# Gated recurrence of a twelve-plus-four sublayer network: weight splits ahead of the next pair's sigmoid, the last pair's output products by column halves, and the next sublayer's first splits during the last mean square

## The reference, cut to what matters

```python
q, zf, zb, i, g = jnp.split(h @ w_in, 5, axis=-1)      # h is the normed x, w_in is 1024 x 5120
k_f, logf_f = forget(zf)                               # forget: a bounded sigmoid of z
k_b, logf_b = forget(zb)
o = forward_scan(q, k_f, v, logf_f) + backward_scan(q, k_b, v, logf_b)    # 8 heads of 128
o = _rms_norm(o, g_norm) * jax.nn.silu(gh)             # the mean square is over one head's 128 features
return o.reshape(B, T, D_MODEL) @ w_out                # w_out is 1024 x 1024
```

## Time and profile before

| what | value |
|---|---|
| launches, median (lowest to highest) | 3114.99 us (3114.23 to 3117.01) |
| the profiled launch: its own time, its span | 3116.85 us, 3115.0 us |
| instructions in the profile | 46410 |
| PE busy | 2902.4 us, 93% of the span |
| PE's share of the chain of work that ended last | 83% (DVE 9%, ACT 4%) |
| DVE busy | 1998.4 us, 64% |
| ACT busy | 1425.0 us, 46% |
| mean granted clock of PE over the span | 0.964 of full |
| the two recurrences, from the first pair's first score to the last product with `w_out` | 193.0 us and 192.9 us |

### The profile page before, as it was taken

How to read it: one execution, slowest core, us unless ns; L and a number is a source line. 1 busy time by engine, 2 the same in 40 slices (tenths; PEclk the granted TensorE clock), 3 DMA queues, 4 the chain that set the end, 5 groups by cost and what they waited for, 6 DMA issues and landing times.

```text
span 3115.0 us, 46410 instructions
## 1 busy us (share of the span) xinstructions
PE 2902.4 (93%) x19567; PEld 2643.7 (85%) x19567; DVE 1998.4 (64%) x2593; ACT 1425.0 (46%) x1891; POOL 83.2 (3%) x135
## 2 busy tenths in 40 slices
PE   7999889999989999999799999997999789896998
PEld 7999879999976999995489999986899689794897
DVE  5657766566657656553665665677666677746777
ACT  4445544444444444442554444554444445343453
POOL 0000000000011000000000000000000000000000
PEclk9999989999999999999999999998999889997999
DMA  6554336575532655642146566432564455542552
GB/s 231 183 163 136 115 97 201 176 216 183 160 104 61 214 186 183 184 117 86 61 141 185 169 198 188 149 122 89 163 185 157 157 165 176 163 150 81 163 188 97
DMA packets 404051, 478.24 MB, mean 154 GB/s; under 512 B 16394, under 2 KB 331492, under 8 KB 403844
## 3 DMA queue, kind: packets, MB, share of 16 engines
q1 hardware_dynamic: 400432, 467.33, 48.0%
q0 software_dynamic: 1776, 6.77, 0.8%
q10 hardware_dynamic: 1636, 1.18, 0.1%
HBM read 474.17 MB, written 1.05 MB: 153 GB/s over the span
## 4 chain that ended last, share of the span: by engine, by line
PE 83%; DVE 9%; ACT 4%; issue 3%; ACTq 0%; DVEq 0%
PE Wk L569 16%; PE Wk L571 16%; PE Wk L570 16%; PE Y L569 9%; PE Y L570 9%; PE Y L571 9%; DVE w_lo L1608 2%; PE Wk L577 2%; DVE work L1846 2%; ACT w_hi L1133 1%; PE Y L926 1%; PE Y L681 1%; PE Wk L899 1%; PE Y L829 1%; PE Wk L915 1%
## 5 line engine op out<-in xcount | busy, mean ns | idle before, releaser
L1608 DVE TENSOR_TENSOR w_lo<-ring,w_hi 128x1024 fp32r<-128x1024 f32 x872 | 1046.8, 1223 | 680.5 <-ACT w_hi L1133 634.2
L569 PE MATMUL Wk<-xT_hi,w_hi 128*128 128x256 f32 x4320 | 1234.3, 286 | 19.2 <-DVE xT_lo L1646 16.0
L571 PE MATMUL Wk<-xT_hi,w_lo 128*128 128x256 f32 x4320 | 1226.3, 284 | 0.0
L570 PE MATMUL Wk<-xT_lo,w_hi 128*128 128x256 f32 x4320 | 1226.3, 284 | 0.0
L1133 ACT ACTIVATE w_hi<-ring 128x1024 fp32r<-128x1024 f32 x872 | 896.6, 1053 | 644.4 <-PE Wk L571 432.6
L569 PEld LDWEIGHTS Wk<-xT_hi,w_hi 128*128 128x128 f32 x4320 | 832.9, 193 | 26.5 <-issue 13.0
L570 PEld LDWEIGHTS Wk<-xT_lo,w_hi 128*128 128x128 f32 x4320 | 833.0, 193 | 4.7 <-issue 0.9
L571 PEld LDWEIGHTS Wk<-xT_hi,w_lo 128*128 128x128 f32 x4320 | 832.6, 193 | 0.0
L569 PE MATMUL Y<-w_hi,hid_hi 128*128 128x512 f32 x896 | 352.4, 393 | 4.3 <-DVE hid_lo L1700 4.3
L570 PE MATMUL Y<-w_lo,hid_hi 128*128 128x512 f32 x896 | 351.0, 392 | 0.0
L571 PE MATMUL Y<-w_hi,hid_lo 128*128 128x512 f32 x896 | 349.8, 390 | 0.0
(11 more groups left out here) (250 smaller groups left out, 2796.9 us busy)
## 6 DMA issues: line engine op xcount, KB each, us to landing
ring<-in_ffn_w_gu SPq DMA_DIRECT2D x352, 512.0 KB, 4.4
ring<-in_ffn_w_down SPq DMA_DIRECT2D x224, 512.0 KB, 4.4
ring<-in_ffn_w_up SPq DMA_DIRECT2D x96, 512.0 KB, 6.0
ring<-in_hg_w_in SPq DMA_DIRECT2D x80, 512.0 KB, 3.6
ring<-in_na_w_in SPq DMA_DIRECT2D x24, 512.0 KB, 4.5
ring<-in_hg_w_out SPq DMA_DIRECT2D x16, 512.0 KB, 3.7
ring<-in_lru_w_in SPq DMA_DIRECT2D x16, 512.0 KB, 4.0
ring<-in_kv_w SPq DMA_DIRECT2D x16, 512.0 KB, 4.7
```

Source lines behind the costliest of these rows:

```text
L569: pe.matmul(o, l_hi, r_hi, start=first, stop=False)
L570: pe.matmul(o, l_hi, r_lo, start=False, stop=False)
L571: return pe.matmul(o, l_lo, r_hi, start=False, stop=last)
L1608: dve.tensor_tensor(lo, raw(u), hi.bitcast(F32), ALU.subtract).then_inc(lo_done, 1)
```

## The change

Six things are edited, all for the recurrence:

1. On ACT and DVE, in pairs 0 to 2, `ahead` moves from the end of a round to just after the scores' own steps: on ACT before `squares_of`, `roots`, `z_sigmoid`, `one_minus` and `save_values`, on DVE before `save_z`, `save_q`, `bounded` and `both_ways`. `g_sigmoid`, `gate_of` and, on DVE, `normed` still stand ahead of it. How many units are split by each round stays the same.
2. In the last pair the units are split by a table, `HALVES_LAST`: up to unit 42 + (0, 0, 1, 1, 2, 2, 3, 4, 5) by rounds 0 to 8, where it was up to 44, 45, 46 and 47 by rounds 0 to 3.
3. `pair_out` goes by column halves, into rounds 0, 2, 4, 6: (pair 0, n 0), (pair 1, n 0), (pair 0, n 1), (pair 1, n 1). The order of loads and units follows. Only n = 1 now waits for `normed` of pair 2.
4. Pairs 0 and 1 are split into `hid_hi` and `hid_lo`, buffers that the recurrence doesn't use otherwise. Pair 0 is split in round 5 of pair 2, pair 1 in round 0 of the last pair, pair 2 in round 5.
5. `squares_of` of pair 2 stands at the head of round 1 on ACT (it stood after `g_sigmoid`), and the sum goes to bank 0 instead of bank 4.
6. After the last round ACT and DVE split three units of the next sublayer, before the last pair's squares and norm. DVE no longer runs `splits(end[s] + 1)` ahead of the residual, so it takes the fourth unit in the feed-forward block, behind the wait for `r_ready`.

```diff
-MS_BANKS = (4, 4, 4, 2)
+MS_BANKS = (4, 4, 0, 2)
+HALVES_LAST = (0, 0, 1, 1, 2, 2, 3, 4, 5)
@@ units_of
+        if subs[s][0] == "hg":
+            order[-8:-4] = [(t1 - 4, 0), (t1 - 3, 0), (t1 - 4, 1), (t1 - 3, 1)]
@@ tensor, hgrn
-                    if p_ + 1 < HG_PAIRS:
+                    if p_ + 2 < HG_PAIRS:
                         pe.wait_ge(g_saved, Q + 2)
+                    elif p_ + 1 < HG_PAIRS:
+                        pe.wait_ge(q_saved, Q + 2)
...
-                    if j == 0 and n == 0:
-                        pe.wait_ge(g_saved, Q0 + HG_PAIRS)
-                        pe.wait_ge(o_ready, Q0 + HG_PAIRS - 1)
-                    y_half(out_of(base[s] + 5 * HG_PAIRS, j), n, first=j == 0)
+                    if j == 0:
+                        pe.wait_ge(*((o_ready, Q0 + HG_PAIRS - 1) if n else (g_saved, Q0 + HG_PAIRS)))
+                    t = base[s] + 5 * HG_PAIRS
+                    a = (t + j, pair_of(hid_hi, j), pair_of(hid_lo, j)) if j < 2 else out_of(t, j)
+                    y_half(a, n, first=j == 0)
...
-                        if last and 3 <= i < 7:
-                            pair_out((i - 3) // 2, (i - 3) % 2)
+                        if last and i in (0, 2, 4, 6):
+                            pair_out(i // 2 % 2, i // 4)
@@ scalar, hgrn
+                        if last and i == 1:
+                            squares_of(p_ - 1)
                         if i < LEVELS - 1:
                             facing_keys(p_, i + 1)
...
-                        if p_ and i == 3 - 2 * last:
+                        if not last:
+                            ahead(HALVES_AHEAD + 10 * (p_ + 1) + i, s)
+                        if p_ and i == 3 and not last:
                             squares_of(p_ - 1)
...
-                        ahead(HALVES_AHEAD + 10 * (p_ + 1) + i, s)
+                        else:
+                            ahead(HALVES_AHEAD + 38 + HALVES_LAST[i], s)
+                ahead(10 * HG_PAIRS + 10, s, over=True)
                 squares_of(HG_PAIRS - 1)
@@ vector, hgrn
-                        if last and i in (1, 2):
-                            split_pair(i - 1)
+                        if p_ == HG_PAIRS - 2 and i == 5:
+                            split_pair(0)
+                        if last and i in (0, 5):
+                            split_pair(1 + i // 5)
                         if p_ and i == 6 - 3 * last:
                             normed(p_ - 1)
-                            if last:
-                                split_pair(2)
                         if not last:
+                            ahead(HALVES_AHEAD + 10 * (p_ + 1) + i, s)
                             if i == 4:
                                 save_z(p_ + 1)
...
-                        ahead(HALVES_AHEAD + 10 * (p_ + 1) + i, s)
+                        else:
+                            ahead(HALVES_AHEAD + 38 + HALVES_LAST[i], s)
+                ahead(10 * HG_PAIRS + 10, s, over=True)
                 normed(HG_PAIRS - 1)
@@ vector, the loop over sublayers
-                splits(end[s] + 1)
+                if kind != "hg":
+                    splits(end[s] + 1)
```

More of the change, by code:

```diff
@@ L339, in other_block, with pair_of @@
             return bass.AP(a.tensor, a[:, at:at + 1].offset, [list(a.ap[0]), [2, m // 2], [half, 2], [0, B]])
+        def pair_of(a, j):
+            return a[:, j, :].rearrange("p (k t) -> p k t", k=2)
         def r_wide(m, np_=P):
@@ L1139, in splits, with ahead @@
                     nxt[0] += 1
-            def ahead(n, s):
-                while nxt[0] <= nth[split_units_of(s)[0]] + n and split_units[nxt[0]][0] < end[s]:
+            def ahead(n, s, over=False):
+                while nxt[0] <= nth[split_units_of(s)[0]] + n and (over or split_units[nxt[0]][0] < end[s]):
                     high(split_units[nxt[0]])
@@ L1870, in split_pair @@
                     dve.wait_ge(o_ready, Q0 + pp + 1)
-                    split_out(2 * pp, 2, hg_o[:, pp, :], (o_high, Q0 + pp + 1), o_split)
+                    if pp >= 2:
+                        split_out(2 * pp, 2, hg_o[:, pp, :], (o_high, Q0 + pp + 1), o_split)
+                        return
+                    dve.tensor_copy(hid_hi[:, pp, :], hg_o[:, pp, :]).then_inc(o_high, 1)
+                    dve.wait_ge(o_high, Q0 + pp + 1)
+                    dve.tensor_tensor(hid_lo[:, pp, :], hg_o[:, pp, :], hid_hi[:, pp, :].bitcast(F32), ALU.subtract)\
+                        .then_inc(o_split, 1)
                 splits(base[s] + 2)
```

## The result

The changed kernel took 3072.3 us (median of four launches, 3071.3 to 3075.9), the kernel before 3115.8 us in the same comparison: a ratio of 0.9862, with a 95% interval of 0.9847 to 0.9878. That is 43.5 us, where 33.8 were predicted. The same kernel in a later comparison took 3072.5 us.

What follows compares the result with a forecast made beforehand. Bound by PE (TensorE busy 93% of the span) except where PE waits; 2.0 + 3.1 + 3.1 + 8.0 + 3.2 - 2.5 = 16.9 us a recurrence, 33.8 us for both, gave 3081 us, range 3071 to 3097.

Steps and rivals of the forecast that it cites:

- Pairs 1 and 2: Splits first in these pairs' rounds: scores of rounds 6 and 7 come earlier, 3.1 us for each pair.
- The walk: Step-by-step timing of the new instruction order through the recurrence's queues, using earlier trace durations and taking full clock.
- Pair 0: Splits first in pair 0: 2.8 us at full clock, 1.2 at half clock, taken as 2.0 us.
- `split_pair(0)` and `both_ways`: Pair 2's split in DVE idle time and splits ahead of round 8's `both_ways`: no cost, the latter without margin.
- the slower rival: Next pair's first score waits for `both_ways` behind round 8's splits: 3123 us at 7 us late, 4 in 100.
- The last pair: New order up to its output: 6 to 9.7 us, taken as 8.0 us a recurrence.
- Hand-over: Next sublayer's splits before the last pair's norm, none ahead of the residual: +3.2 us a recurrence.
- fourth unit: DVE splits it behind `r_ready`, PE idle 1.75 us plus possible half clock: -2.5 us a recurrence.
- The cover: After the output, ACT's four copies ahead of the squares are hidden by PE's work, by 0.1 us.
- Short waits keep the clock down: Last pair at 0.50 clock throughout, nothing left of its 8.0 us: 8.9 us each, 3097 us, 11 in 100.
- A longer line in the last pair: Products before scores lengthen rounds, half of the 8.0 us comes: 12.9 us each, 3089 us, 15 in 100.
- Full clock: Everything in the recurrence lands at full clock: 20.2 us each, 3074.6 us, 12 in 100.

Runs made afterwards that it cites:

- e6: Changed kernel with ACT's squares put back ahead of the split of round 3 in pairs 1 and 2: 3077.4 us, ratio 0.9874.
- e1: Kernel before with edit 1 alone (splits earlier in the rounds of pairs 0 to 2): 3092.0 us, ratio 0.9927.
- e10: Changed kernel with unused matmuls of constants added before scores 4 (four) and 8 (three) of the last pair: 3070.1 us, ratio 0.9856.
- e11: Changed kernel with e9's table, hand-over and fourth-unit edit plus e10's added matmuls: 3067.4 us, ratio 0.9842.
- e4: Changed kernel with DVE splitting the next sublayer's fourth unit directly after the residual: 3072.4 us, ratio 0.9861.
- e7: Changed kernel with pair 2's squares put back behind the gate's sigmoid in round 1 of the last pair: 3076.1 us, ratio 0.9871.
- e3: Kernel before with edits 2 to 5 alone (the last pair's new order): 3092.2 us, ratio 0.9928.
- e5: Changed kernel with the last pair's split table as (0, 0, 0, 0, 1, 2, 3, 4, 5): 3072.3 us, ratio 0.986.
- e12: Changed kernel timed once more, unedited, beside e9 to e11: 3072.5 us, ratio 0.9859.
- e8: Changed kernel with both the table of e5 and the fourth-unit edit of e4: 3070.8 us, ratio 0.9856.
- e9: Changed kernel with e4's edit, table (0, 0, 0, 0, 1, 2, 2, 3, 4) and two instead of three next-sublayer units ahead: 3068.1 us, ratio 0.9846.

## Why the prediction was right, and where its sizes were off

**Pairs 1 and 2: mechanism right, 4.3 and 4.2 us instead of 3.1.** The walk had PE idle for 0.8 us before round 6 and about 0.4 us before round 7, and there was none. Round 5 to 6 took 351.72 - 347.78 = 3.94 us where the walk had 4.6, round 6 to 7 took 3.9 where it had 4.3. The wait before round 8 was as walked, 0.7 us. Two things made the walk too long. It started the line of round 4 from where it stood in the earlier trace rows, but in round 3 the squares (0.6 us of ACT) now stand behind the split, so DVE's part came 0.5 us sooner; e6 shows that this is worth 0.47 us a pair. And it added full durations, where instructions of ACT and DVE in a row overlap: `facing_keys` starts at 351.03 and takes 0.63, and the next `w_hi` starts at 351.57. That 0.09 us, four or five times in a line, would be some 0.4 us of the 0.6 that remain; no run tested it, and the rest is open.

**Pair 0: 2.98 us instead of 2.0.** I had taken a mean between full clock (2.8) and half clock (1.2). The idle time that is left, 1.50 us instead of 2.94, brought no fall in either recurrence (stretches at 1.00), so the full-clock case was the right one.

**`split_pair(0)` and `both_ways`: no cost, as costed.** Pair 2 took 41.22 us with that split and 41.07 without it (e1): 0.15 us, next to nothing. PE came to the first score of the last pair at 367.07 without idle time, so nothing was late where the slower rival had its place.

**The last pair: the waits right, the falls of the clock mis-sized.** The walk put scores 1 to 4 at 5.5, 9.1, 12.9 and 16.6 us and the start of product 3 at 18.7; they came at 5.41, 9.18, 12.96, 16.54 and 18.73. The wait before score 4, walked as 3 us, was 2.53. At full clock it gave the output at 32.8 us. An estimate from the rows above for the changed kernel without a fall is 18.7 + 2.85 + 10.75 = 32.3 us, so the order is worth 10.2 us and not 9.7. That e10 came out at 32.95 and 32.99 us and e11 at 32.80 is no proof of the 32.8: e10 holds some 0.65 us that the filling itself costs, and e11 has another table.

The falls are where the sizes were off. I took them as lasting 3 to 4 us, from the 0.50 in 400.27 to 404.50 of the earlier trace rows. That stretch was only the end of a longer fall in the kernel before:

```profile
394.99:405.23 10.24, 4.96 (x12) 3.93 (x13) 6.11 (x10) 0.77 (x2) 0.00 (x0) 0.50 0.17 53
```

After the change the fall behind score 4 lasted 6.8 us in the first recurrence and 3.4 in the second, and the pair was 35.02 and 33.71 us: 2.7 and 1.4 us over the estimate, where I had taken off 1.7 for two. What I hadn't put in the sum is that one more can come at the output: 3.56 us instead of 1.99 for it, which is the 1.54 us of the stretch behind. From scale to scale the whole stretch took 227.1 and 227.3 us before, 206.3 and 203.4 after, 202.7 and 202.7 with the filling. So the filling, its own cost included, gave back 3.6 and 0.7 us.

**Hand-over: +3.4 and +3.5 instead of +3.2; fourth unit: -2.0 instead of -2.5.** ACT's four copies lay in front of the squares (done at 405.72 + 0.59), and PE came to their sum at 408.23. The cover that I had put at 0.1 us (by the walk's own figures, a start at 4.2 and 0.6 us against PE at 4.6, it was missing by 0.2) was 1.9 us in this recurrence, where the output was slow, and 0.4 in the second, where it wasn't. The four copies took 3.9 us and began 0.16 us before the output. The wait was 1.73 us (1.75 predicted) and no fall followed it, so the 0.75 us that I had added for one were not there. It cost 2.0 us from scale to scale, 0.26 more than the wait; that rest is open. e4 took it away in the stretch.

**The rivals.** "Short waits keep the clock down" needed 0.50 throughout the last pair; it was 0.90 and 0.95. By the rule of the Trainium skill that I set beside it ("TensorE: Matmul & The Clock Gate", "A second HAM failure mode: psum-queue depth-cycling"), gaps between groups of matmuls make the clock swing. I had read it as this rival's time, but the page speaks of a swing between the two levels and not of the low one throughout. The traces agree with the swing (0.50 in 384.81:391.63, 1.00 in 2133.62:2144.37). By the estimate above it cost 2.7 + 1.5 us in the first recurrence and 1.4 in the second, where the rival leaves nothing of the last pair's gain. "A longer line in the last pair" had half of 8.0 us for the pair; it gave 7.45 and 8.91, and the scores up to the fourth came when the walk had them. "Full clock" was right for all terms but the falls; its 3074.6 us were still above the result, because pairs 1 and 2 and pair 0 gave more.

**What went well for no good reason.** That 16.9 us a recurrence came near 18.8 is in part luck: pairs 0 to 2 gave 3.3 us more than walked, and from the last pair's first score to the last tile the first recurrence gave 2.1 us less than the 8.0. Of the 9 us between prediction and result, the terms hold 40.7 - 33.8 = 6.9. Most of the rest is between profiled launches and medians, 40.9 and 43.5 us.

**Open.** How the last pair's gain divides between the column halves, the table and the new buffers: only the squares were moved alone (e7), and e3 has all of it together. Why e4 shows no gain in total. Whether e7's median launches had fewer falls than its profiled one, as I suppose. Differences of 2 to 4 us between kernels lie within what the falls of the clock do from launch to launch, and four or five launches don't resolve them.

## What to carry to other kernels

In an in-order queue, work that needs nothing goes in front of the instruction that waits, not behind it: moving the splits that way gave 23.3 us by itself (the whole change gave 43.5), and one 0.6 us instruction in the wrong place left PE idle for 4.4 us (e7). A line of short waits is walked at full clock, and the fall of the clock is then a term of its own, behind the longest wait and for longer than one product (6.8 us here, once); where that wait can't be shortened, matmuls of constants into a free bank held the clock at 1.00 here, and they must be no longer than the wait. When a wait is shortened, look where the same line makes PE wait next (e5: four rounds on), and read small edits in their own stretch, since launches differ by as much as they bring.

## What the runs showed of the hardware

**Half clock behind waits of 1.4 to 2.5 us.** Waits of PE of 2.4 to 2.5 us before score 4 and of 0.9 to 1.0 us before product 3 stood in ten last pairs (after, e4, e6, e7, e12, two each). In all ten product 3 took 4.25 to 5.26 us instead of 2.85. In e3, with the same 2.53 us before score 4, the clock fell at once: score 4 took 2.08 and 1.86 us instead of 1.16 and product 3 took 4.74 and 3.53. With the first wait at 1.45 us (e5, e8, e9) it took 2.85 us in two and 4.4 us in four. With the first wait filled (e10) it took 2.82 and 2.85 us. So shortening a wait from 2.5 to 1.45 us wasn't enough, and filling it was. In the ten the output took 3.5 to 3.6 us in the eight where the product had taken 5.25, and 1.99 us in the two where it had taken 4.3. That one decides the other isn't shown, and the other kernels speak against it: in e5 and e8 the output took 3.61 and 3.47 us behind a product at full clock, and in e3 1.99 us behind one of 4.74. No run here tells when the second fall comes.

The Trainium skill ("TensorE: Matmul & The Clock Gate", "What's actually happening") tells of a clock that activity holds up and idleness lets fall. The traces agree with both: 1.00 in the last pairs with the waits before scores 4 and 8 filled (e10), 0.90 and 0.95 without.

**Identical parts differ by the clock.** The same attention sublayer, untouched by any edit, in three kernels (columns as in the earlier trace rows); the first is the changed kernel:

```profile
798.11:976.44 178.33, 160.76 (x918) 126.04 (x917) 117.24 (x184) 83.01 (x158) 24.86 (x37) 0.92 0.31 97
```

The kernel before:

```profile
816.87:993.48 176.61, 157.43 (x918) 124.87 (x917) 117.03 (x184) 83.00 (x158) 24.82 (x37) 0.94 0.31 97
```

The kernel with the fourth unit's wait removed (e4):

```profile
796.38:971.14 174.76, 154.59 (x918) 123.72 (x917) 116.94 (x184) 82.99 (x158) 24.84 (x37) 0.96 0.32 98
```

The same 918 matmuls took 178.33, 176.61 and 174.76 us at 0.92, 0.94 and 0.96. Nearly 4 us of a launch's time are decided there by where the clock falls, as much as the fourth unit's edit was to bring.
